# Block transposes on VectorE in place of transposed products, and preparation moved to the head of a unit, in a chunked delta-rule recurrence

## The reference, cut to what matters

```python
def step(S, inp):
    w_t, k_t, v_t, kk_t, a_t = inp[:5]
    sa = jnp.einsum('bhvk,bhk->bhv', S, -kk_t)
    S = (S * w_t[:, :, None, :] + sa[..., None] * (kk_t * a_t)[:, :, None, :]
         + v_t[..., None] * k_t[:, :, None, :])
    y = jnp.einsum('bhvk,bhk->bhv', S, inp[5]) if len(inp) == 6 else None
    return S, y
```

## Time and profile before

| | us |
|---|---|
| median of three runs | 4052.66 |
| the profiled execution, its own time | 4049.61 |
| its span, from the first to the last instruction | 4047.8 |
| PE busy / weight loads / DVE / ACT / POOL | 3586.4 / 2666.9 / 1590.9 / 1017.6 / 1061.3 |
| mean granted clock of TensorE | 0.937 of full speed |
| the 16 units, from the first score on PE to the last unit's last product | 2709 to 3557 |

### The profile page before, as it was taken

One profiled execution on the slowest core, in us unless ns is written; L12 is line 12 of the kernel. 1 busy time (PEld: TensorE's weight loads), 2 busy tenths in 40 slices (PEclk: granted clock), 3 DMA queues, 4 the chain that ended last, 5 costly groups with the idle time before them and its releaser, 6 DMA issues.

```text
span 4047.8 us, 84008 instructions
## 1 busy us (share of the span) xinstructions
PE 3586.4 (89%) x37130; PEld 2666.9 (66%) x37130; DVE 1590.9 (39%) x2806; ACT 1017.6 (25%) x1590; POOL 1061.3 (26%) x696
## 2 busy tenths in 40 slices
PE   8996798778868899989999989859999999989997
PEld 3454476623326677768888845438888888867885
DVE  3255542411127755433333420314555455523333
ACT  2032232211114244331111031322322332223221
POOL 0002341121122100032222120025555454424441
PEclk9997899889979899989999989979999999989998
DMA  4207153179961100111111123420000000011221
GB/s 172 94 32 294 44 207 127 74 277 369 362 249 37 42 1 1 69 79 63 63 63 63 63 76 132 157 73 3 14 14 14 14 14 14 4 63 73 100 98 42
DMA packets 64600, 379.35 MB, mean 94 GB/s; under 512 B 12906, under 2 KB 12906, under 8 KB 26352
## 3 DMA queue, kind: packets, MB, share of 16 engines
q1 hardware_dynamic: 40032, 291.52, 18.7%
q0 software_dynamic: 20608, 68.82, 4.4%
q10 hardware_dynamic: 3600, 13.63, 0.9%
HBM read 380.21 MB, written 44.04 MB: 105 GB/s over the span
## 4 chain that ended last, share of the span: by engine, by line
PE 75%; DVE 6%; POOL 6%; DMA 6%; ACT 3%; issue 2%; SPq 0%; DVEq 0%; ACTq 0%; POOLq 0%
PE psum L462 20%; PE psum L474 11%; PE psum L475 10%; PE psum L476 10%; PE psum L750 4%; DMA arena<-in_wall 3%; PE psum L2096 2%; PE psum L2827 2%; PE psum L2814 2%; PE psum L769 2%; PE psum L2123 2%; DMA ring<-in_wall 2%; PE psum L648 1%; PE psum L3116 1%; PE psum L2797 1%
## 5 line engine op out<-in xcount | busy, mean ns | idle before, releaser
L462 PE MATMUL psum<-arena 64*64 64x64 f32 (+4 forms) x14024 | 636.6, 235 | 57.1 <-POOL arena L3050 23.5
L462 PEld LDWEIGHTS psum<-arena 64*64 64x64 f32 (+2 forms) x14024 | 511.3, 139 | 151.2 <-issue 109.9
L492 POOL TENSOR_TENSOR ring_low<-ring,slab_high 128x2048 fp32r<-128x2048 f32 x66 | 303.9, 4617 | 648.7 <-ACT slab_high L485 648.6
L474 PE MATMUL psum<-h_high,slab_high 128*128 128x512 f32 (+1 forms) x1056 | 378.1, 358 | 16.6 <-DVE h_low L512 10.0
L475 PE MATMUL psum<-h_low,slab_high 128*128 128x512 f32 (+1 forms) x1056 | 376.9, 357 | 0.0
L476 PE MATMUL psum<-h_high,ring_low 128*128 128x512 f32 (+1 forms) x1056 | 376.5, 356 | 0.0
L462 PE MATMUL psum<-arena,ring 128*128 128x512 f32 (+3 forms) x992 | 368.4, 531 | 2.1 <-DVEq L1269 1.3
L462 PEld LDWEIGHTS psum<-arena,ring 128*128 128x128 f32 (+2 forms) x992 | 184.2, 187 | 184.0 <-issue 173.5
L474 PEld LDWEIGHTS psum<-h_high,slab_high 128*128 128x128 f32 x1056 | 201.4, 191 | 51.8 <-issue 10.6
L941 DVE TENSOR_TENSOR arena<-arena,psum 128x512 f32<-128x512 f32 x66 | 39.5, 599 | 486.1 <-PE psum L476 481.9
L476 PEld LDWEIGHTS psum<-h_high,ring_low 128*128 128x128 f32 x1056 | 201.5, 191 | 28.4
(11 more groups left out here) (433 smaller groups left out, 6241.1 us busy)
## 6 DMA issues: line engine op xcount, KB each, us to landing
ring<-in_wall SPq DMA_DIRECT2D x181, 1024.0 KB, 5.1
arena<-in_wall SPq DMA_DIRECT2D x96, 1024.0 KB, 12.1
moe_rows<-arena POOLq DMA_DIRECT2D x2, 6144.0 KB, 67.7
arena<-moe_rows ACTq DMA_DIRECT2D x24, 512.0 KB, 7.7
moe_out<-arena POOLq DMA_DIRECT2D x24, 512.0 KB, 9.1
arena<-spill POOLq DMA_DIRECT2D x8, 1024.0 KB, 5.3
spill<-arena POOLq DMA_DIRECT2D x2, 3072.0 KB, 17.7
filters<-arena POOLq DMA_DIRECT2D x2, 2048.0 KB, 6.6
```

Source lines behind the costliest of these rows:

```text
L462: last = L.eng.matmul(out, a, b, start=(i == 0), stop=(i == len(pairs) - 1))
L474: L.eng.matmul(out, a_hi, b_hi, start=(i == 0), stop=False)
L492: L.eng.tensor_tensor(m.low[:, n % SLOTS, :], m.ring[:, n % SLOTS, :], m.high_of(n).bitcast(F32), ALU.subtract).then_inc(m.sem("slab_split ...
```

## The change

1. `transposed_tensor` runs on the last level only. At the others DVE, when it has updated a head's `ti`, writes its transpose into `tt` with its own transpose instruction (`inverse_turn_vector`), which turns each block of 32 by 32 where it lies. Up to level 16 the inverse has nothing outside those blocks. The second kind of score (`al` by `be`) goes too, with its mask: the starting `ti` is turned from the `tt` that POOL writes. POOL writes `tt` only (four operations instead of six).
2. `FIRST` is 8, so the last chain steps, four instead of two, run between the turns of `al` and `be`, one behind each half turn.
3. The next unit's gates are made at the head of a unit, ahead of the wait for `prepared`, and their sigmoids are ACT's first work there. The sums of the norm follow the sixth score, its turn follows the read-out's sums ahead of the levels. DVE makes reciprocal and running sum after the chain, ahead of the read-out's centring, and no longer after level 4.
4. POOL takes key times gain ahead of the start of the inverse, and the decay's sums ahead of the key's product. The norm uses `u.ka` as its scratch, and no longer `B.cm`.

The core of the diff (bank counting that follows from it is left out):

```diff
 def gates_scalar(L, m, B, u):
     if u.n > 0:
-        L.eng.wait_ge(m.sem("prepared"), L.nth("prepared"))
+        L.eng.wait_ge(m.sem("decay_sum"), u.n)
...
 def prepare_pool(L, m, B, u):
+    decay_sum_pool(L, m, B, u)
     if u.d == 0:
-        removal_raw_pool(L, m, B, u)
         removal_key_pool(L, m, B, u)
-    decay_sum_pool(L, m, B, u)
     keys_pool(L, m, B, u)
...
+def inverse_turn_vector(L, m, dst, src, hh):
+    L.eng.transpose(heads_columns(dst, hh), heads_columns(src, hh)).then_inc(m.sem("inverse_turned"), 1)
+    return L.nth("inverse_turned")
...
-FIRST = 10
+FIRST = 8
 def unit_tensor(L, m, B, u, before, done, after, w2, g2):
+    if after is not None:
+        gates_tensor(L, m, B, after, w2)
     L.eng.wait_ge(m.sem("prepared"), L.nth("prepared"))
...
-    for lhs, rhs, n in ((u.be, u.al, TT), (u.al, u.be, TT), (u.ka, u.al, TT), (u.be, u.rh, TX), (u.ka, u.rh, TX)):
+    for lhs, rhs, n in ((u.be, u.al, TT), (u.ka, u.al, TT), (u.be, u.rh, TX), (u.ka, u.rh, TX)):
...
+        if after is not None and after.d == 0 and at_bank == 6:
+            removal_sum_tensor(L, m, B, after)
...
-        for tiles in TURNS:
+        for half, tiles in enumerate(TURNS):
             turned.append(turn_pair_tensor(L, m, src, tiles))
-        if before is not None and k < 2:
-            chain_tensor(L, m, B, before, FIRST + k)
+            if before is not None and k < 2:
+                chain_tensor(L, m, B, before, FIRST + 2 * k + half)
...
     if after is not None and after.d == 0:
-        removal_sum_tensor(L, m, B, after)
+        removal_turn_tensor(L, m, B, after)
...
         for hh in range(2):
             L.eng.wait_ge(*corner[hh])
-            inverse[hh] = []
-            if lv != LEVELS[-1]:
-                inverse[hh].append(inverse_tensor(L, B, hh))
-            inverse[hh].append(transposed_tensor(L, B, hh))
-        if lv == LEVELS[0]:
-            if after is not None and after.d == 0:
-                removal_turn_tensor(L, m, B, after)
-            if after is not None:
-                gates_tensor(L, m, B, after, w2)
+            if lv != LEVELS[0]:
+                L.eng.wait_ge(m.sem("inverse_turned"), L.nth("inverse_turned"))
+            inverse[hh] = inverse_tensor(L, B, hh) if lv != LEVELS[-1] else transposed_tensor(L, B, hh)
...
 def unit_vector(L, m, B, u, before, done, after):
...
+    turned_back = []
+    for hh in range(2):
+        L.eng.wait_ge(m.sem("inverse_begun"), L.nth("inverse_begun"))
+        turned_back.append(inverse_turn_vector(L, m, B.ti, B.tt, hh))
+    if after is not None and after.d == 0:
+        removal_inverse_vector(L, m, removal_rooted)
+    if after is not None:
+        decay_scan_vector(L, m, B, after)
     if done is not None:
         readout_centre_vector(L, m, B, done)
...
+            if lv != LEVELS[-1]:
+                L.eng.wait_ge(*L.read_out)
+                turned_back[hh] = inverse_turn_vector(L, m, B.tt, B.ti, hh)
```

More of the change, by code:

```diff
@@ L3227, in copy @@
         L.eng.activation(dst, src, ACT.Copy, scale=scale).then_inc(L.bank_free, 1)
[L3229 removed]
+    if after is not None:
+        gates_scalar(L, m, B, after)
+    for _ in range(6 * (1 if before is None else 2)):
+        L.next_bank()
+    if after is not None and after.d == 0:
+        removal_square_scalar(L, m, B, after)
+        removal_root_scalar(L, m, B, after)
+    for _ in range((FIRST - 6) * (1 if before is None else 2)):
         L.next_bank()
@@ L3258, in unit_scalar @@
             L.next_bank()
-        for _ in range(4 if lv != LEVELS[-1] else 2):
+        for _ in range(2):
             L.next_bank()
-        if lv == LEVELS[0]:
-            if after is not None and after.d == 0:
-                removal_spread_scalar(L, m, B, after)
-                removal_turn_scalar(L, m, B, after)
-            if after is not None:
-                gates_scalar(L, m, B, after)
     if after is not None:
@@ L3300, in unit_vector @@
     first, upto = MASK["before"][d], MASK["upto"][d]
+    if after is not None:
+        L.next_bank(2)
+        L.next_bank(2)
     if before is not None:
@@ L3308, in unit_vector @@
     for hh in range(2):
-        ti_read = read(of_head(B.ti, hh), masked(4 + d))
+        read(of_head(B.akt, hh), masked(first))
         chain(2 + hh)
-        L.eng.wait_ge(*ti_read)
-        L.eng.sem_inc(m.sem("starts_read"), 1)
-    for hh in range(2):
-        read(of_head(B.akt, hh), masked(first))
-        chain(4 + hh)
     for k, dst in enumerate((B.rbt, B.rkt)):
@@ L3318, in unit_vector @@
             read(of_head(dst, hh, TX), masked(upto))
-            chain(6 + 2 * k + hh)
+            chain(4 + 2 * k + hh)
+        if after is not None and after.d == 0 and k == 0:
+            L.next_bank()
+            removal_rooted = L.read_out
     if u.d == 0:
@@ L3323, in unit_vector @@
     for k in range(3):
-        L.next_bank()
-        L.next_bank()
-        if k < 2:
-            chain(FIRST + k)
+        for half in range(2):
+            L.next_bank()
+            if k < 2:
+                chain(FIRST + 2 * k + half)
+    turned_back = []
+    for hh in range(2):
+        L.eng.wait_ge(m.sem("inverse_begun"), L.nth("inverse_begun"))
+        turned_back.append(inverse_turn_vector(L, m, B.ti, B.tt, hh))
+    if after is not None and after.d == 0:
+        removal_inverse_vector(L, m, removal_rooted)
+    if after is not None:
+        decay_scan_vector(L, m, B, after)
     if done is not None:
```

76 lines of the change are left out of this document (35 added, 41 removed).

## The result

The changed kernel takes **4014.7 us** (median of 4 runs, 4004.1 to 4016.1) against 4052.4 for the kernel before (4 runs beside it): ratio 0.990, interval 0.988 to 0.992. It is faster, by 38 us where I forecast 103, and outside my range of 3932 to 3998. The profiled execution took 4013.6 us.

The account below looks back on a forecast made before the run. PE's own stream was taken to set the pace; -90.3 us for seven pairs of units, -7.5 each for units 0 and 15 and +1.9 ahead of unit 0 gave -103.4, so 3949 us, range 3932 to 3998 (0.8).

Parts of the forecast that it names:

- Levels: Inverse levels of an odd unit: DVE's loop of 3.28 us per settled level, 16.0 for 22.3 in all, -6.3.
- My bounds for the transpose: DVE's transpose in the levels: 0.36 at the fastest cast's rate, 0.96 at the running sum's; 0.56 taken.
- Even levels: Levels of an even unit, with about 1.9 us more for the read-out: 17.9 against 24.1, -6.2.
- Scores and turns: Score stage: two wide steps go, -2.0 us; two chain steps between half turns add 0.9 odd, 1.0 even.
- Ahead of the levels: PE waits before the levels: +1.4 us for the late centring in even units, +0.9 for the norm's turn in odd.
- Head: Unit start: gates cover a 0.4 us wait and bring a bank wait of 0.3; -0.4 odd, 0 even.
- Ahead of unit 0: Before the first unit, the key's product on POOL no longer hides behind the running sum: +1.9 us.
- Rivals 2, 3 and 4: Half-rate transpose, 4013 us, 0.10; PE stands for banks at the head, 3994, 0.08; transposes wait for POOL, 4064, 0.05.
- the first rival: The forecast itself, whole kernel: 3934 us with a fast transpose to 3985 with waits at upper bounds; chance 0.76.
- The step that failed: Opening paragraph on the whole kernel: PE's own stream sets the pace, so the change can gain by taking PE work away.
- small term: Per unit: bank wait at the head +0.3 us, centring wait in even units +1.4, norm's sums in odd score stages -0.2.
- My terms: All stages' changes added up per unit: -7.1 us odd, -5.8 even, -7.5 each for units 0 and 15.

Follow-up runs that it names:

- the kernel with the norm put back: The changed kernel with the norm's squares, sums (behind `akv`) and turn (behind the first level) where the kernel before had them: 3983.8 us, ratio 0.984.
- both + solve order: The changed kernel with early sigmoid table load, running sum behind the read-out's centring, and solved products ordered ua, ua, uv, uv: 3966.2 us, ratio 0.980.

## Why the prediction was wrong, point by point

- **Levels**: right. 3.28 us from corner to corner, transpose 0.578 against 0.56, at a clock of 1.00; 16.4 us in unit 3 (2877.93 to 2894.35) for 16.0. Two terms of the loop were off and cancelled, which was luck: no row shows the 0.10 behind a subtraction, in unit 2 the transpose follows after 0.03 (2835.64 + 0.35 to 2836.02), and the next operation starts 0.50 behind a transpose (2836.88 to 2837.38) and not 0.40. My bounds for the transpose are estimates from rows 7 and 10, where a cycle is what a column adds to mask and subtraction, 1.09 ns (0.56 and 0.35 us for 384 and 192 columns): the casts add about half of it, 0.52 (427 and 294 ns for 512 and 256), which makes 0.36 for 384 columns, and the running sum takes about twice as much, 2.3 (1.75 us for 768), which makes some 0.9. In the kernel with the norm put back a whole odd unit takes 46.5 us (3049.68 to 3096.18, gates to gates).
- **Even levels**: 17.9 forecast. Unit 2 took 2842.87 - 2822.85 = 20.0, of which 3.4 at a clock of 0.55, which costs 1.7 at most; so 0.4 or more was mis-sized.
- **Scores and turns**: right, where the clock stood. From the first score to the first turn an odd unit took 2872.06 - 2862.73 = 9.3 before and 7.8 in unit 7 of the kernel with the norm put back (3051.17 to 3058.97), 1.5 less, for a forecast of 2.0 less and 0.3 more of waiting. The turns took 1.0 more there (3058.97 to 3063.72, against 2872.06 to 2875.82), for 0.9.
- **Ahead of the levels**: the wait for the centring came as worked out, 1.55 for 1.4; in odd units PE waits 3.5 / 7 = 0.5 for the norm's turn (L2897), for 0.9. **Head**: the bank wait was there, 0.2 to 0.8 for my 0.3. POOL was not waited for inside the recurrence. Ahead of unit 0 the first score came 3.4 us later than before (2712.52 for 2709.14), where I had 1.9.
- **Rivals** 2, 3 and 4 fell: transposes from 533 to 580 ns beside a busy POOL (15.3 of 16.4 us in the levels of unit 3); PE's waits for L2976 sum to 4.3 us, not 45. In the first rival the upper bounds of the small terms add up to 2.5 per pair and not 2.1, which changes nothing.
- **The step that failed** is in the prediction's first paragraph: I read the windows of units 4 and 5, PE busy 98.28 of 104 us at a granted clock of 1.00, as a property of the kernel, and priced all that followed at a clock of 1.00. Each small term (+0.3, +1.4, and -0.2 for the sums) was an argument about a microsecond; together they lowered the clock for 131 us of 730 (mean 0.91 for 1.00). The sum had no term for it, and no rival either.

Is that one step enough? From unit 1's gates to unit 14's the kernel with the norm put back took 3393.29 - 2752.04 = 641 us (starts of L2964, the gates, in PE's timeline), at a clock of 0.99, with two waits that belong to the norm's old place: 8.0 us (L2814 above) and seven times 1.43 for the sums outside DVE's loop, 10. Without them 623. My terms give seven odd units of 45.75 and six even ones of 49.1 there, 615. The changed kernel took 3427.42 - 2749.24 = 678. So some 55 of the 63 us missing there go with the clock, by this arithmetic. The other 8 are about the 7.3 us that PE waits for L3360 in that kernel. The changed kernel has no such wait, so nearly all of the 63 may be the clock's there; half of the 131 us at the lower level allows 66. The runs show the cause (the clock falls behind waits added to the kernel before, and returns in the changed kernel when the norm's sums leave the score stage); the split into us is worked out.

There was a sign in the trace of before that I passed over: the clock did fall once in its units, in the score stage of unit 13, behind this (PE's timeline, then windows, of before):

```profile
3407.15 0.39 PE L462 MATMUL psum<-arena 64*64 64x64 f32 x7 [0.83 <-issue]
...
3408.42 0.28 PE L3116 MATMUL psum<-arena 64*64 64x64 f32 x2 [0.30 <-DVE arena L3136]
```

```profile
3395.00:3408.00 13.00, 11.59 (x369) 10.75 (x362) 8.03 (x21) 0.00 (x0) 11.21 (x11) 1.00 0.25 84
3408.00:3416.00 8.00, 7.70 (x98) 6.62 (x95) 2.62 (x10) 1.74 (x4) 2.19 (x2) 0.57 0.01 2
```

The fall stands behind a wait of 0.83 within a score stage (beside a load here too, DMA share 0.25). Longer waits stood elsewhere in the same kernel without a fall, in the levels:

```profile
PE psum L2814 <- DVE arena L3294: 16.6, 20, 1.2
```

The change took these away and made smaller ones in the score stage.

## What to carry to other kernels

Where a change takes work from a PE that is full, ask what the granted clock will do: look in the profile of before for the smallest gap behind which it already fell, and count waits, and groups like the norm's sums, in the stage where PE is paced by another engine. A microsecond of waiting ahead of or in that stage cost up to four or five here (48 us for 10, 119 for 25 to 29), and about one once the norm's sums were out of it (20 for 17). Price a wait by the stage that follows it; an edit that removes one wait can be a loss (24 us here) if it makes the next one appear ahead of a loose stage.

## What was not expected of the hardware

- A gap of 0.6 us more in each unit cost 48 us in all, one of 1.8 us 119: four to five times its length, by falls to a granted clock of 0.50 for up to 27 us.
- The clock can fall behind a group without a wait in it: behind the norm's sums, 1.50 us in which the trace has PE busy. In the score stage a fall followed them in each of seven odd units of the kernel "both + solve order" (0.50 to 0.60); behind `akv`, with the same length, in none of seven (the kernel with the norm put back).
- VectorE's transposes are not held by POOL (533 to 580 ns), but two operations of the read-out that read two tiles in SBUF (L3477 and the bonus) look held. In the kernel with the norm put back L3477, a sum of the read-out, falls beside a product on POOL:

```profile
3025.44 2.27 DVE L3477 SCALAR_TENSOR_TENSOR arena<-arena,vecs 128x512 f32<-128x512 f32 x1
...
3025.34 1.81 POOL L3034 TENSOR_TENSOR arena<-arena 128x768 f32<-128x768 f32 x1
```

It takes 742 to 751 ns in the kernel before (L3469 there), where POOL stands idle beside it. In the changed kernel, where it is L3479, it starts shortly before a product on POOL ends:

```profile
2829.12 1.82 POOL L3034 TENSOR_TENSOR arena<-arena 128x768 f32<-128x768 f32 x1
...
2830.74 0.74 DVE L3479 SCALAR_TENSOR_TENSOR arena<-arena,vecs 128x512 f32<-128x512 f32 x1
```

In both it ends 0.54 to 0.56 us behind the end of POOL's product, so it looks held until that operation is over, whatever its own length. It costs PE up to 1.5 us in an even unit of the kernel with the norm put back (the wait for L3360 above). The bonus (L3459), which also reads two tiles in SBUF, takes 1.86 us in seven of eight units of the changed kernel for 0.75 before. Why these two look held and the transposes do not, no run shows.
